# Token rows as three bf16 parts, subtracted in the banks, and gathered by three bf16 products

## The chip, the cores and the metric

The kernel runs on one core of a Trainium2 chip. The metric is the device time of one execution in microseconds (us). TensorE (PE in the profile) multiplies matrices into eight PSUM banks of 128 x 512 f32. VectorE (DVE), ScalarE (ACT) and GpSimd (POOL) do the elementwise work, and SyncE (SP) issues most of the weight transfers. The engines run side by side and wait for one another by semaphores.

## The reference, cut to what matters

One step of a two-layer encoder over 320 token rows (256 of a prompt, 64 of a sample) with 1024 features. Layer 0 mixes by an RWKV-7 recurrence, layer 1 by windowed attention, and each is followed by a mixture of 32 experts:

```
def per_sequence(t):
    lg = (t @ wg).astype(jnp.float32)                      # 4 groups
    gi = jnp.argmax(lg, axis=-1)
    ...
    tv, ti = lax.top_k(jax.nn.softmax(le, axis=-1), TOP_K) # 2 of the 8 experts of the group
    tw = tv / jnp.sum(tv, axis=-1, keepdims=True) * gp[:, None]
    ...
    gu = jnp.einsum('sd,edf->sef', t, w_gu)
    hid = jax.nn.silu(gu[..., :D_EXPERT]) * gu[..., D_EXPERT:] * cw[..., None].astype(t.dtype)
    return jnp.einsum('sef,efd->sd', hid, w_down)
```

Each token has a weight for two experts only, so 640 pairs of token and expert matter. The change is in the stage that puts the tokens in the order of their experts.

## The kernel before

The kernel is written by hand for each engine: five instruction streams, each in its written order, with a wait wherever one needs another's result. `pe.wait("mask", l)` means that TensorE waits for the instruction that another stream marked with that key. The stage before each expert loop, called the routing stage here, runs once in each layer (`moe(0)`, `moe(1)`) and has the same instructions both times:

- **TensorE** (from L986) sums the squares of the norm, makes the router's logits of the normed tokens `hT` (feature on the partition, token along the row), turns the logits and `hT` to token rows (24 transposes in f32 for `hT`, four into each of six banks: three tiles of tokens, two halves of the features), fills in with `keep_busy(9)` (products into a bank nobody reads; each f32 product is two records in the trace), waits for the mask of the chosen experts, makes the ranks with nine small bf16 products, fills in with `keep_busy(6)`, and then gathers: 16 banks (eight chunks of 128 features, two halves of 320 of the sorted places), in each three f32 products of `htok` (token rows) with `pick` (a 0/1 matrix that says which token goes to which place). After that come `keep_busy(4)` and the expert loop.
- **ScalarE** (from L1377) copies the six banks of turned tokens to `htok` (L1386, through the helper L1255). It writes them in another order of features: the 512 values of a row in the bank go out as 64 groups of 8, each of the 8 to an address 128 elements further. Then it loads the table for Exp, makes the exponentials of the router, and later copies the even chunks of the gathered rows from their banks to `xall`.
- **VectorE** (from L1710) finds group, first and second expert, builds the mask and the ranks, compares a row of numbers with each token's places (`pick`, L1812 to L1819: `is_equal`, then `is_equal` and add, in two halves of 320 places), and copies the odd chunks of the gathered rows to `xall`. When these are there, the expert loop begins.
- **GpSimd** clears the padding of the third token tile (L627), which has 64 tokens only.

PSUM banks are given out in a ring by `Banks.open`: the next bank in turn, after a wait until its last contents were read. One bank at a time can be kept out of the ring (`hold`).

The expert loop that follows takes four experts at a time. Its weights come by SyncE's queue: the first 12 MB are asked for before the routing stage, and each later one when TensorE has used up the place it goes to. The loop's last part, `scatter`, already works with three bf16 parts of each value: 48 bf16 products, each with its own 128 x 128 weights and 320 columns.

Of the kernel before, what the change touches and what calls it, by code (L numbers as in the profile page):

```python
# [31 lines left out]
BF16 = mybir.dt.bfloat16  # L32
# [4 lines left out]
P = 128  # L37
# [182 lines left out]
class Banks:  # L220


    def __init__(self, pe, ps):
        self.pe, self.ps, self.n, self.owner, self.held = pe, ps, 0, [None] * 8, None

    def hold(self, *key):

        self.held = None
        pb = self.open(*key)
        self.held = (self.n - 1) % 8  # L230
        return pb

    def open(self, *key):
        if self.n % 8 == self.held:
            self.n += 1
        b = self.n % 8
        self.n += 1
        if self.owner[b] is not None:
            self.pe.wait("read", *self.owner[b])
        self.owner[b] = key  # L240
        self.pe.seen.bank[key] = b
        return self.ps[b]


def build(nc, i, o, known, seen):
    ctx = ExitStack()
    with ctx:
# [93 lines left out]
        htok = work[:, off[0]:off[0] + 3 * D].rearrange("p (j d) -> p j d", j=3)  # L341
        hrow = htok.rearrange("p j (c q) -> p j q c", c=C)
        dpart = wk(3 * D, BF16).rearrange("p (u s d) -> p u s d", u=2, s=3)
        pick = work[:, off[0]:off[0] + 3 * ROWS].rearrange("p (j s) -> p j s", j=3)
# [11 lines left out]
        ident16 = wk(P // 2, BF16)  # L356
        triu16 = wk(P // 2, BF16)
# [237 lines left out]
        def _(eng):  # L595
# [27 lines left out]
            def cleared(l):  # L623

                pl.wait("ms ready", f"B{l}")
                eng.wait_ge(in_sems["out_written"], outs[0])
                pl.did(eng.memset(htok[64:128, 2, :], 0.0), ("htok padded", l))  # L627
# [52 lines left out]
        def _(eng):  # L680
# [26 lines left out]
            def mod_step(n):  # L707
# [3 lines left out]
                if n < MSTEPS:  # L711
                    g, c = divmod(n, C)
                    if c == 0:
                        bank.hold("mod", g)
                    eng.wait_ge(in_sems[f"modw_in{n % 2}"], 16 * (n // 2 + 1))
                    pe.did(mod_rows(ps[seen_bank(("mod", g))], c, mw[n % 2]), ("mod used", n), ("mod", g))
                elif n == MSTEPS:
                    bank.held = None
# [267 lines left out]
            def moe(l):  # L986
# [10 lines left out]
                for j, (t0, k) in enumerate(TILES):  # L997
                    for hf in range(2):
# [7 lines left out]
                        pb = bank.open("htok", l, j, hf)  # L1006
                        for cc in range(4):
                            ins = eng.transpose(pb[0:k, P * cc:P * cc + P], hT[:, 4 * hf + cc, t0:t0 + k], ident)
                        full(ins, "htok", l, j, hf)
                keep_busy(9)  # L1010
                pe.wait("mask", l)
                pb = bank.open("rank", l)
# [7 lines left out]
                keep_busy(6)  # L1020
                for hf in range(2):
                    for c in range(C):
                        pb = bank.open("rows", l, c, hf)
                        for j, (t0, kt) in enumerate(TILES):
                            if c == 0:
                                if hf == 0:
                                    pe.wait("htok ready", l, j, 1)
                                    if j == 2:
                                        pe.wait("htok padded", l)
                                pe.wait("picked", l, hf, j)  # L1030
                            ins = mm(pb[:, 0:T], htok[:, j, P * c:P * c + P], pick[:, j, T * hf:T * hf + T],
                                     j == 0, j == 2)
                        full(ins, "rows", l, c, hf)
# [212 lines left out]
        def _(eng):  # L1246
# [130 lines left out]
            def moe(l):  # L1377
# [6 lines left out]
                for j, (t0, k) in enumerate(TILES):  # L1384
                    for hf in range(2):
                        act(hrow[0:k, j, 64 * hf:64 * hf + 64, :],  # L1386
                            pk("htok", l, j, hf)[0:k, :].rearrange("p (q c) -> p q c", c=C), ACT.Copy,
                            ("read", "htok", l, j, hf), ("htok ready", l, j, hf))
# [3 lines left out]
                act(rt[:, 36, 0:3], rt[:, 35, 0:3], ACT.Exp, ("route exp", l))  # L1392
                for hf in range(2):
# [106 lines left out]
        def _(eng):  # L1500
# [209 lines left out]
            def moe(l):  # L1710
# [9 lines left out]
                op(eng.tensor_copy(ident16[:, :], cst("ident")))  # L1720
                op(eng.tensor_copy(triu16[:, :], cst("triu")))
# [313 lines left out]
```

## Time and profile before

| | us |
|---|---|
| median of 3 runs | 1304.3 (1299.38 to 1305.35) |
| the profiled execution, its own time | 1300.34 |
| its span in the trace | 1298.6 |
| gather of token rows, layer 0: first to last product | 535.10 to 561.10 |
| the same, layer 1 | 999.65 to 1025.65 |

The trace counts from the start of the span. Each row of the timeline gives the start, the length and the number of instructions that were merged into it, and in brackets how long the engine had been idle before it and what released it. A matmul in f32 is two records, in bf16 one. TensorE works 87% of the span, VectorE 42%, ScalarE 26%, and TensorE's mean granted clock is 0.949 of full speed.

### The profile page before, as it was taken

The page shows a single profiled execution, that of the slowest core. Times are in us where ns is not written, and L with a number is a line of the kernel's source. Part 1 is how long each engine was busy: PE and PEld are TensorE (multiplying, and loading weights), DVE is VectorE, ACT ScalarE, POOL GpSimd, SP SyncE. Part 2 cuts the span into 40 slices and gives each one's busy share as a digit, 9 for nine tenths or more (in the row PEclk, how much of TensorE's full clock was granted, in tenths as well). Part 3 has the DMA queues.
Part 4 walks back from the last instruction along what each step waited for, and adds up shares of the span by engine and source line. Part 5 has one row for each costly group of instructions (what it writes and reads, how often), then busy time and mean ns, then how long its engine had stood idle before and what let it go on. Part 6 is the DMA issues. An engine that isn't in the chain of part 4 may idle for free.

```text
span 1298.6 us, 22252 instructions
## 1 busy us (share of the span) xinstructions
PE 1134.0 (87%) x8975; PEld 655.4 (50%) x8975; DVE 540.4 (42%) x1419; ACT 341.0 (26%) x650; POOL 56.4 (4%) x66
## 2 busy tenths in 40 slices
PE   5579997877788879999999998899798999999985
PEld 2146665554456745644444444566575544444433
DVE  3421194424431254524444444424337244444443
ACT  1122240121111201223333323134213233333322
POOL 2000000000000000000100000000000000001000
PEclk9689998988988979999999999999798999999997
DMA  9533214877874144029999996201540099999941
GB/s 248 180 130 123 72 65 171 292 261 274 282 251 172 39 189 194 1 114 419 422 427 425 422 424 234 95 13 51 210 162 33 9 424 422 425 424 425 418 169 41
DMA packets 45971, 297.11 MB, mean 229 GB/s; under 512 B 5956, under 2 KB 7336, under 8 KB 22344
## 3 DMA queue, kind: packets, MB, share of 16 engines
q1 hardware_dynamic: 43856, 290.17, 56.4%
q0 software_dynamic: 1840, 5.79, 1.9%
q8 instruction: 58, 0.95, 0.3%
q14 instruction: 17, 0.14, 0.0%
q10 hardware_dynamic: 200, 0.06, 0.0%
HBM read 293.77 MB, written 2.24 MB: 228 GB/s over the span
## 4 chain that ended last, share of the span: by engine, by line
PE 75%; DMA 11%; DVE 8%; ACT 3%; issue 2%; SPq 0%; ACTq 0%; DVEq 0%; POOL 0%; POOLq 0%
PE bank L686 73%; DMA ring<-in_ada_w 10%; DVE work L1511 2%; ACT work L1255 2%; DMA ring<-in_kv_ada_w 1%; DVE work L1517 1%; DVE work L1514 1%; DVE rstd L1549 1%; DVE x_res L1883 1%; DMA ring<-in_rw_w_rkv 1%; PE bank L1073 1%; DVE work L1869 1%; DVE ring L1511 1%; DVE work L1623 0%; PE bank L1241 0%
## 5 line engine op out<-in xcount | busy, mean ns | idle before, releaser
L686 PE MATMUL bank<-ring,work 128*64 128x512 f32 (+1 forms) x1600 | 342.9, 582 | 9.3 <-DVE work L1869 7.6
L686 PE MATMUL bank<-work,ring 128*128 128x320 f32 (+3 forms) x1600 | 302.3, 368 | 24.6 <-DVE work L1511 8.8
L686 PEld LDWEIGHTS bank<-work,ring 128*128 128x128 f32 (+2 forms) x1600 | 214.1, 173 | 112.2 <-issue 23.9
L686 PE MATMUL bank<-work 128*128 128x320 bf16 (+7 forms) x1906 | 223.6, 283 | 20.3 <-DVE x_res L1883 7.7
L686 PEld LDWEIGHTS bank<-ring,work 128*64 128x64 f32 (+1 forms) x1600 | 113.3, 137 | 212.0 <-issue 205.0
L686 PEld LDWEIGHTS bank<-work 128*128 128x128 bf16 (+3 forms) x1906 | 164.9, 125 | 91.0 <-issue 25.1
L1255 ACT ACTIVATE work<-bank 128x320 f32<-128x320 f32 (+6 forms) x111 | 55.4, 540 | 237.1 <-PE bank L686 220.9
L686 PE MATMUL bank<-ring,cs 128*32 128x512 f32 x448 | 66.0, 680 | 49.2 <-DMA ring<-in_ada_w 42.2
L1883 DVE SCALAR_TENSOR_TENSOR x_res<-bank,mod,x_res 128x256 f32<-128x256 f32 (+1 forms) x256 | 86.2, 378 | 16.7 <-PE bank L686 2.8
L1863 DVE SCALAR_TENSOR_TENSOR work<-work,small,bank 128x256 f32<-128x256 f32 x32 | 21.5, 672 | 170.4 <-ACT work L1419 89.2
L1255 ACT ACTIVATE ring<-bank 128x512 f32<-128x512 f32 (+3 forms) x67 | 37.7, 563 | 189.9 <-PE bank L686 188.8
L686 PEld LDWEIGHTS bank<-ring 64*64 64x64 f32 (+2 forms) x1984 | 74.5, 146 | 25.4 <-issue 21.7
L686 PE MATMUL bank<-ring 64*64 64x64 f32 (+2 forms) x1984 | 84.3, 237 | 3.5 <-issue 3.5
L1876 DVE TENSOR_TENSOR work<-bank,work 128x512 f32<-128x512 f32 x64 | 44.1, 689 | 61.9 <-ACT work L1423 61.9
L640 POOL TENSOR_TENSOR work<-work 128x512 bf16<-128x512 f32 x32 | 36.4, 1160 | 539.4 <-ACT work L1427 539.4
L1423 ACT ACTIVATE work<-bank 128x512 bf16<-128x512 f32 x64 | 38.1, 596 | 49.3 <-PE bank L686 49.3
L686 PEld LDWEIGHTS bank<-ring,cs 128*32 128x32 f32 x448 | 10.3, 113 | 77.3 <-DMA ring<-in_ada_w 59.0
L1517 DVE SCALAR_TENSOR_TENSOR work<-work,vec 128x320 f32<-128x320 f32 x56 | 27.0, 548 | 52.5 <-PE bank L686 52.2
L1511 DVE TENSOR_TENSOR ring<-ring,const_phase 128x512 f32<-128x512 f32 x30 | 20.4, 679 | 58.5 <-PE bank L686 58.3
L1407 ACT COPY work<-work 128x512 f32 x64 | 39.3, 623 | 14.1 <-issue 14.1
L1427 ACT ACTIVATE work<-work 128x512 bf16<-128x512 f32 x64 | 40.1, 626 | 8.6 <-DVE work L1876 8.6
L1255 ACT ACTIVATE work<-x_res 128x640 f32<-128x640 f32 x20 | 14.7, 737 | 98.3 <-DVE x_res L1517 46.7
(189 smaller groups left out, 816.8 us busy)
## 6 DMA issues: line engine op xcount, KB each, us to landing
ring<-in_moe_w_gu SPq DMA_DIRECT2D x64, 2048.0 KB, 13.4
ring<-in_moe_w_down SPq DMA_DIRECT2D x64, 1024.0 KB, 14.2
ring<-in_ada_w SPq DMA_DIRECT2D x40, 1024.0 KB, 5.0
ring<-in_rw_w_rkv SPq DMA_DIRECT2D x6, 2048.0 KB, 7.9
ring<-in_ada_w SPq DMA_DIRECT2D x4, 2048.0 KB, 28.9
ring<-in_kv_ada_w SPq DMA_DIRECT2D x8, 1024.0 KB, 5.5
ring<-in_rw_w_o SPq DMA_DIRECT2D x2, 2048.0 KB, 11.2
ring<-in_at_w_q SPq DMA_DIRECT2D x2, 2048.0 KB, 14.1
```

What stands on the lines that cost most here:

```text
L640: eng.tensor_tensor(dpart[:, 0, 2, cols], rest[:, n, :], dpart[:, 0, 1, cols], ALU.subtract).then_inc(S["lo_ready0"], 1)
L686: return eng.matmul(out, l, r, start=start, stop=stop, **kw)
L1073: ins = eng.transpose(ps[0][:, 2 * P * u + P * f:2 * P * u + P * f + P], hid[:, u, P * f:P * f + P], ident)
L1255: ac.did(eng.activation(out, in_, f, **kw), *keys)
L1407: eng.copy(xe[:, u, :, 64 * v:64 * v + 64], xall[:, :, bass.ds(at, SLOTS)]).then_inc(S["xe_ready"], 1)
L1423: eng.activation(dpart[:, u, 0, 512 * n:512 * n + 512], ps[4 + n][:, :], ACT.Copy).then_inc(S["hi_ready"], 1)
L1427: eng.activation(dpart[:, u, 1, 512 * n:512 * n + 512], rest[:, n, :], ACT.Copy).then_inc(S["mid_ready"], 1)
L1511: op(eng.tensor_tensor(out, a, b, o_), *keys)
L1517: op(eng.scalar_tensor_tensor(out, a, s_, b, o1, o2), *keys)
L1863: eng.scalar_tensor_tensor(hid_w[:, u], silu[:, u, :].rearrange("p (q f) -> p q f", f=2), wslot[:, u:u + 1], ps[3 + 4 * u][:, FE:2 * FE].r ...
L1876: eng.tensor_tensor(rest[:, n, :], ps[4 + n][:, :], dpart[:, u, 0, 512 * n:512 * n + 512], ALU.subtract).then_inc(S["rest_ready"], 1)
L1883: ins = eng.scalar_tensor_tensor(x[:, c, t0:t0 + n], ps[(6, 1, 2)[c % 3]][:, t0:t0 + n], mod[:, l, r, 40 + c:40 + c + 1], x[:, c, t0:t0 + ...
```

## The change

The token rows are no longer kept in f32 (`htok`), but as three bf16 parts (`hpart[0..2]`) whose sum is the f32 value to the last bits. ScalarE copies each bank of turned tokens to the first part. TensorE then adds minus the part to the same bank (a product of `minus16`, minus the identity in bf16, with the part in the feature order of the bank), so that the bank holds what is left, and ScalarE copies that to the second part; once more the same for the third. The six banks stay out of the ring until the gather. `pick` is bf16, and each gathered bank is the sum of nine bf16 products (three parts, three token tiles) in place of three in f32; the products go four banks at a time, part by part.

```diff
--- before.py
+++ after.py
@@ -221,17 +221,16 @@
 
 
     def __init__(self, pe, ps):
-        self.pe, self.ps, self.n, self.owner, self.held = pe, ps, 0, [None] * 8, None
+        self.pe, self.ps, self.n, self.owner, self.held = pe, ps, 0, [None] * 8, set()
 
     def hold(self, *key):
 
-        self.held = None
         pb = self.open(*key)
-        self.held = (self.n - 1) % 8
+        self.held.add((self.n - 1) % 8)
         return pb
 
     def open(self, *key):
-        if self.n % 8 == self.held:
+        while self.n % 8 in self.held:
             self.n += 1
         b = self.n % 8
         self.n += 1
@@ -338,10 +337,12 @@
         wk(B)
         xall = wk(C * RP).rearrange("p (c s) -> p c s", c=C)
 
-        htok = work[:, off[0]:off[0] + 3 * D].rearrange("p (j d) -> p j d", j=3)
-        hrow = htok.rearrange("p j (c q) -> p j q c", c=C)
+        hpart = [t.bitcast(BF16).rearrange("p (j d) -> p j d", j=3) for t in
+                 (work[:, off[0]:off[0] + 3 * D // 2], work[:, off[0] + 3 * D // 2:off[0] + 3 * D],
+                  work[:, B:B + 3 * D // 2])]
+        hrow = [t.rearrange("p j (c q) -> p j q c", c=C) for t in hpart]
         dpart = wk(3 * D, BF16).rearrange("p (u s d) -> p u s d", u=2, s=3)
-        pick = work[:, off[0]:off[0] + 3 * ROWS].rearrange("p (j s) -> p j s", j=3)
+        pick = work[:, off[0]:off[0] + 3 * ROWS // 2].bitcast(BF16).rearrange("p (j s) -> p j s", j=3)
         rest = wk(D).rearrange("p (n d) -> p n d", n=2)
         silu = wk(2 * FE).rearrange("p (u f) -> p u f", u=2)
         hid = wk(2 * FE).rearrange("p (u f) -> p u f", u=2)
@@ -354,6 +355,7 @@
         cw = wk(3 * EXP).rearrange("p (j e) -> p j e", j=3)
         cwpart = wk(3 * 3 * EXP // 2, BF16).rearrange("p (s j e) -> p s j e", s=3, j=3)
         ident16 = wk(P // 2, BF16)
+        minus16 = wk(P // 2, BF16)
         triu16 = wk(P // 2, BF16)
         ones16 = wk(P // 2, BF16)
         msk16 = wk(3 * EXP // 2, BF16).rearrange("p (j e) -> p j e", j=3)
@@ -624,7 +626,8 @@
 
                 pl.wait("ms ready", f"B{l}")
                 eng.wait_ge(in_sems["out_written"], outs[0])
-                pl.did(eng.memset(htok[64:128, 2, :], 0.0), ("htok padded", l))
+                for t in hpart:
+                    pl.did(eng.memset(t[64:128, 2, :], 0.0), ("htok padded", l))
 
             def low_parts(l):
 
@@ -711,11 +714,12 @@
                 if n < MSTEPS:
                     g, c = divmod(n, C)
                     if c == 0:
+                        bank.held.clear()
                         bank.hold("mod", g)
                     eng.wait_ge(in_sems[f"modw_in{n % 2}"], 16 * (n // 2 + 1))
                     pe.did(mod_rows(ps[seen_bank(("mod", g))], c, mw[n % 2]), ("mod used", n), ("mod", g))
                 elif n == MSTEPS:
-                    bank.held = None
+                    bank.held.clear()
 
             def keep_busy(n):
 
@@ -1003,13 +1007,26 @@
                                 ins = eng.transpose(pb[0:k1, 36 * jj:36 * jj + 36], lgT[0:36, t1:t1 + k1],
                                                     ident[0:36, 0:36])
                             full(ins, "logits tok", l)
-                        pb = bank.open("htok", l, j, hf)
+                        pb = bank.hold("htok", l, j, hf)
                         for cc in range(4):
-                            ins = eng.transpose(pb[0:k, P * cc:P * cc + P], hT[:, 4 * hf + cc, t0:t0 + k], ident)
+                            ins = mm(pb[0:k, P * cc:P * cc + P], hT[:, 4 * hf + cc, t0:t0 + k], ident, cc == 0,
+                                     cc == 3, is_transpose=True)
                         full(ins, "htok", l, j, hf)
-                keep_busy(9)
+
+                def without(part):
+
+                    for j, (t0, k) in enumerate(TILES):
+                        for hf in range(2):
+                            pe.wait("hpart", l, part, j, hf)
+                            full(mm(ps[seen_bank(("htok", l, j, hf))][0:k, :], minus16[0:k, 0:k],
+                                    hrow[part][0:k, j, 64 * hf:64 * hf + 64, :], False, True,
+                                    skip_group_check=True), "hless", l, part, j, hf)
+
+                pe.wait("minus", l)
+                without(0)
+                keep_busy(6)
                 pe.wait("mask", l)
-                pb = bank.open("rank", l)
+                pb = bank.hold("rank", l)
                 for j in range(3):
                     for jj in range(j + 1):
                         ins = mm(pb[:, EXP * j:EXP * j + EXP], triu16[:, :] if jj == j else ones16[:, :],
@@ -1017,20 +1034,27 @@
                 for jj in range(3):
                     ins = mm(pb[:, 96:96 + EXP], ones16[:, :], msk16[:, jj, :], jj == 0, jj == 2)
                 full(ins, "rank", l)
-                keep_busy(6)
+                without(1)
+                keep_busy(3)
+                rank_bank = seen_bank(("rank", l))
+                bank.held.clear()
+                bank.held.add(rank_bank)
+                pe.wait("htok padded", l)
                 for hf in range(2):
-                    for c in range(C):
-                        pb = bank.open("rows", l, c, hf)
-                        for j, (t0, kt) in enumerate(TILES):
-                            if c == 0:
-                                if hf == 0:
-                                    pe.wait("htok ready", l, j, 1)
-                                    if j == 2:
-                                        pe.wait("htok padded", l)
-                                pe.wait("picked", l, hf, j)
-                            ins = mm(pb[:, 0:T], htok[:, j, P * c:P * c + P], pick[:, j, T * hf:T * hf + T],
-                                     j == 0, j == 2)
-                        full(ins, "rows", l, c, hf)
+                    for c4 in (0, 4):
+                        pbs = [bank.open("rows", l, c, hf) for c in range(c4, c4 + 4)]
+                        for part in range(3):
+                            for c in range(c4, c4 + 4):
+                                for j in range(3):
+                                    if c % 4 == 0:
+                                        pe.wait("hpart", l, part, j, 1)
+                                        pe.wait("picked", l, hf, j)
+                                    ins = mm(pbs[c % 4][:, 0:T], hpart[part][:, j, P * c:P * c + P],
+                                             pick[:, j, T * hf:T * hf + T], part == 0 and j == 0,
+                                             part == 2 and j == 2)
+                                if part == 2:
+                                    full(ins, "rows", l, c, hf)
+                bank.held.clear()
                 keep_busy(4)
                 pe.wait("passes", l)
                 for b in range(8):
@@ -1381,15 +1405,25 @@
                 modulated(f"B{l}", hT, hT)
                 act(lgT[0:36, :], pk("logits", l)[0:36, 0:T], ACT.Copy, ("read", "logits", l), ("logits ready", l))
                 eng.wait_ge(in_sems["out_written"], (64, 144)[l])
-                for j, (t0, k) in enumerate(TILES):
-                    for hf in range(2):
-                        act(hrow[0:k, j, 64 * hf:64 * hf + 64, :],
-                            pk("htok", l, j, hf)[0:k, :].rearrange("p (q c) -> p q c", c=C), ACT.Copy,
-                            ("read", "htok", l, j, hf), ("htok ready", l, j, hf))
+
+
+                def parts(n):
+                    for j, (t0, k) in enumerate(TILES):
+                        for hf in range(2):
+                            if n:
+                                ac.wait("hless", l, n - 1, j, hf)
+                            last = [("read", "htok", l, j, hf)] if n == 2 else []
+                            act(hrow[n][0:k, j, 64 * hf:64 * hf + 64, :],
+                                pk("htok", l, j, hf)[0:k, :].rearrange("p (q c) -> p q c", c=C), ACT.Copy,
+                                ("hpart", l, n, j, hf), *last)
+
+                parts(0)
                 ac.wait("group max", l)
                 ac.wait("top2", l)
                 act(rt[:, 6:9, 0:4], rt[:, 3:6, 0:4], ACT.Exp)
                 act(rt[:, 36, 0:3], rt[:, 35, 0:3], ACT.Exp, ("route exp", l))
+                parts(1)
+                parts(2)
                 for hf in range(2):
                     for c in range(0, C, 2):
                         act(xall[:, c, T * hf:T * hf + T], pk("rows", l, c, hf)[:, 0:T], ACT.Copy,
@@ -1718,6 +1752,7 @@
                 op(eng.memset(msk16[64:128, 2, :], 0.0))
                 op(eng.memset(before[:, 0:1], 0.0))
                 op(eng.tensor_copy(ident16[:, :], cst("ident")))
+                ts(minus16[:, :], cst("ident"), -1.0, None, M, ALU.bypass, ("minus", l))
                 op(eng.tensor_copy(triu16[:, :], cst("triu")))
                 op(eng.tensor_copy(ones16[:, :], cst("ones")))
                 eng.wait_ge(in_sems["out_written"], (64, 144)[l])
```

## Rows read from the trace of the kernel before

**Rows 1.** Page, part 1 and part 4: busy time of each engine, and the chain that ended last.
```profile
PE 1134.0 (87%) x8975; PEld 655.4 (50%) x8975; DVE 540.4 (42%) x1419; ACT 341.0 (26%) x650; POOL 56.4 (4%) x66
...
PE 75%; DMA 11%; DVE 8%; ACT 3%; issue 2%; SPq 0%; ACTq 0%; DVEq 0%; POOL 0%; POOLq 0%
```

**Rows 2.** Chain of waits, layer 0's routing stage (start us, us, what).
```profile
520.33 4.55 ACT work L1255 x5
...
525.86 1.28 ACT L1255
...
527.15 0.32 ACT work L1255 x2
...
529.86 31.26 PE bank L686 x117
...
561.14 0.49 DVE work L1834
```

**Rows 3.** Timeline, layer 0's routing stage: start us, us, engine, line, what.
```profile
509.39 0.95 POOL L627 MEMSET work<- 64x1024 f32 x1 [59.10 <-DVE rstd L1514]
...
518.49 0.22 DVE L1722 CAST work<-const 128x128 bf16<-128x128 f32 x1
...
520.33 5.51 ACT L1255 ACTIVATE work<-bank 128x512 f32<-128x512 f32 x6 [0.22 <-PE bank L1008]
...
521.04 0.23 DVE L1729 COPY work<-bank 128x72 f32<-128x72 f32 x1 [0.44 <-PE bank L1003]
...
522.67 5.01 PE L686 MATMUL bank<-const 128*128 128x320 f32 x18
...
529.86 0.39 PE L686 MATMUL bank<-work 128*128 128x32 bf16 x9 [2.18 <-DVE work L1790]
...
530.10 5.17 PE L686 MATMUL bank<-const 128*128 128x320 f32 x12
...
533.45 1.48 DVE L1517 SCALAR_TENSOR_TENSOR work<-work 128x320 f32<-128x320 f32 x3
...
535.10 26.00 PE L686 MATMUL bank<-work 128*128 128x320 f32 x96
...
536.92 0.44 ACT L1255 ACTIVATE work<-bank 128x320 f32<-128x320 f32 x1 [9.46 <-PE bank L686]
```

**Rows 4.** Groups by form, 519 to 562 us: shapes, count, busy us, mean ns.
```profile
L1255 ACT ACTIVATE work<-bank 128x512 f32<-128x512 f32 x4 | 3.7, 1085 | 0.2 <-PE bank L1008 0.2
...
L1255 ACT ACTIVATE work<-bank 64x512 f32<-64x512 f32 x2 | 2.0, 1086 | 0.0
```

**Rows 5.** Timeline, beginning and first rounds of layer 0's expert loop.
```profile
563.78 2.19 ACT L1407 COPY work<-work 128x512 f32 x4
...
588.73 0.63 ACT L1407 COPY work<-work 128x512 f32 x1 [0.20 <-issue]
...
591.10 0.60 ACT L1423 ACTIVATE work<-bank 128x512 bf16<-128x512 f32 x1 [0.43 <-PE bank L686]
...
597.86 6.69 PE L686 MATMUL bank<-work 128*128 128x320 bf16 x48
```

**Rows 6.** Timeline, layer 1's routing stage.
```profile
991.70 0.31 ACT L1255 ACTIVATE work<-work 128x12 f32<-128x12 f32 x2
...
999.65 26.00 PE L686 MATMUL bank<-work 128*128 128x320 f32 x96
```

**Rows 7.** Windows of 1 us: share of busy time (instructions) of each engine, TensorE's granted clock, DMA.
```profile
531.00:532.00 1.00, 1.00 (x4) 0.72 (x3) 0.90 (x6) 0.00 (x0) 0.00 (x0) 0.64 0.00 0
532.00:533.00 1.00, 1.00 (x3) 0.61 (x3) 0.93 (x5) 0.00 (x0) 0.00 (x0) 0.50 0.00 0
533.00:534.00 1.00, 1.00 (x4) 0.61 (x3) 0.96 (x4) 0.00 (x0) 0.00 (x0) 0.50 0.00 0
534.00:535.00 1.00, 1.00 (x4) 0.72 (x3) 1.00 (x3) 0.00 (x0) 0.00 (x0) 0.65 0.00 0
535.00:536.00 1.00, 1.00 (x5) 0.68 (x5) 0.96 (x4) 0.00 (x0) 0.00 (x0) 1.00 0.00 0
```

## The prediction

> **What bounds the kernel now.** I read the page first: TensorE is busy 87% of the span, and three quarters of the chain that ended last are its own [rows 1]. A faster gather on TensorE can therefore pay, if nothing else comes to stand before it. Next the chain of waits through the routing stage of layer 0 [rows 2]: ScalarE's copies of the turned tokens, its table load and its exponentials lead to the mask, and from 529.86 the chain stays on TensorE for 31.26 us, until VectorE copies the last gathered bank at 561.14. Of these 31.26 us the gather is 26.00 (535.10 to 561.10), 96 records for 48 f32 products [rows 3]. Layer 1 has the same 26.00 us, from 999.65 [rows 6]. What follows (fillers, VectorE's selection, the expert loop) hangs on the gather's end. The refills of the loop's weights are asked for when TensorE has used a place up, so they move with it; the first 12 MB were asked for before this stage, and the window rows show the transfers silent here [rows 7]. So what the end of the gather gains or loses is gained or lost by the program, twice.
>
> When can the gather begin? Before, with the last `pick` of its first half: VectorE's compare-and-add ends at 534.93 [rows 3], and the first product starts at 535.10. The fillers ahead of it end there too, since TensorE's clock was at half in part of this stretch [rows 7]. ScalarE has nothing to do from its exponentials (527.47) to 536.92 [rows 2, 3]. This gap is what the change uses.
>
> **The gather's products.** 144 bf16 products of 320 columns take the place of 48 in f32. The nearest rows are those of the loop's scatter: the same shape, each with its own 128 x 128 weights, 48 in 6.69 us [rows 5], so 0.139 us each. 144 x 0.139 = 20.1 us against 26.0: 5.9 us less in each layer. Bounds: below, 320 columns cannot be had for less than the record of an f32 product costs per column (26.00 / 96 = 0.271 us for two passes, so 0.135 and 19.5 us); above, if a step from bank to bank every three products cost something that scatter (six to a bank) does not show, I allow 0.15 and 21.6 us. I take 0.139.
>
> **The parts on ScalarE.** Before there are six copies from bank to `htok`, 5.51 us in all, one 1.09 us long [rows 3, 4]; so the start of each follows the last one's by (5.51 - 1.09) / 5 = 0.88 us. A copy of as many values to consecutive addresses takes 0.60 us [rows 5], so the scattered order (groups of eight, 128 elements apart) costs 0.49. The first part's six copies stay where they are. Twelve more come behind the exponentials, which end at 527.15 + 0.32 = 527.47 [rows 2]. Each writes bf16 in the same scattered order. No row has that. From below: the pace of consecutive writes, (2.19 - 0.63) / 3 = 0.52 us [rows 5]; from above: twice the pace now, 1.77, if a two-byte write to a place of its own costs more than a four-byte one. I take 0.88, since the addresses are as scattered as before and bf16 to consecutive addresses costs no more or less than f32 [rows 5].
>
> The Trainium skill (ScalarE: Activation LUTs, What ACT_TABLE_LOAD costs) gives an ACTIVATE with immediate operands as 186 ns + 0.833 ns a column for fp32 and bf16 alike, which is 613 ns for 512. The trace agrees for consecutive writes (0.60) and not for scattered ones (1.09). By the page ten copies would be done after some 5.3 us, and the gather would wait for `pick` as before.
>
> How many of the twelve stand before the gather? The six banks are held, and `rows` opens four banks before its first product. In the ring's order from the first held bank: two `htok` banks, the logits' bank (taken by `rank`, still held), four `htok` banks, one free. The first four opened are thus the `htok` banks of tiles 0 and 1, and each waits until its third part was read. So the gather begins with the tenth of the twelve copies: 527.47 + 9 x 0.88 + 1.09 = 536.5, with 0.05 for the semaphore 536.55. That is 1.45 later than before. The last two copies (to 538.3) are needed only by the third part, after 24 products or 3.3 us (539.9): hidden. Later groups of four find banks read long before, the nearest being chunk 0's, full nine products (1.25 us) before its group ends against a copy of 0.44.
>
> **TensorE between.** The six subtractions of the first part follow ScalarE's copies at their pace and end soon after 525.84; then six fillers (12 records at 5.01 / 18 = 0.28) until 529.5. TensorE goes on with the mask at 529.86 [rows 3]. The next six subtractions stand behind `rank` (530.25) and follow the copies of the second part, the last at some 532.9; three fillers, to 534.8. All before 536.5, hidden with 1.7 us to spare. If this cover goes, each microsecond costs one.
>
> **The rest, at nothing.** `minus16` is one VectorE instruction (0.22) before a stretch in which VectorE waits 0.44 in layer 0 [rows 3]. Three GpSimd memsets for one of 0.95 at 509.39 end by 512.3, more than 20 us before their wait. `pick` in bf16: same instructions over 320 columns; should they be slower, 1.6 us lie between 534.93 and 536.5. ScalarE's new waits for the second and third part have the Exp of the router ahead of them, not behind, and behind them only the even chunks of the gather, which come later. No DMA is added or moved.
>
> **The sum.** Layer 0's gather ends at 536.55 + 20.1 = 556.65, against 561.10: 4.45 less. In layer 1 the exponentials end at 992.01 [rows 6], and the same steps give 1001.1 + 20.1 = 1021.2 against 1025.65: 4.45. Together 8.9 us. The profiled execution took 1300.34 (span 1298.6 and 1.7 around it), so it becomes 1291.4. The median of the three runs is 4.0 above that execution, with nothing to tell the two kernels apart in this, so I take the loss from the median: 1304.3 - 8.9 = 1295.4.
>
> **Rivals.**
> - **Clock.** TensorE was granted half its clock (1.2 GHz) from 531.3 to 534.7, after it had stood idle for 2.18 us before `rank`; the four windows add up to 1.7 us of lost work [rows 7], now hidden behind `pick`. With the change TensorE has thin work from 530 to 533 (six subtractions) and nothing from 534.8 to 536.5. If such a stretch falls on the gather, each costs 1.7 us. One in each layer: 8.9 - 3.4 = 5.5 us, 1298.8, hardly told from no change.
> - **Fast scattered bf16.** ScalarE's copies at the pace of consecutive writes: the gather begins with `pick` at 535.0 and the gain is 5.9 - 0.0 in each layer, 11.8: 1292.5.
> - **Slow reads on TensorE.** The subtraction's moving operand is the part in scattered order, 256 bytes from one value to the next. No row has such a read. If it went at ScalarE's scattered pace (0.88 us for 512), the second set would end at 530.25 + 5.3 = 535.5, the fillers at 537.2: 0.65 lost in each layer, gain 7.6, 1296.7. At twice that, the set would end at 540.9, the gather would begin at 542.5, and the program would be 3 us slower. The Trainium skill (SBUF — State Buffer, Door 1: The DMA port swizzle, its note on cachelines) says that each access that crosses to a new 16-byte line pays; by it these reads pay at every value, which is why this rival has a chance of its own. No row here shows the size of it.
> - **Slow scattered bf16 (slower).** ScalarE's twelve copies at 1.77: the tenth ends at 527.47 + 9 x 1.77 + 2.2 = 545.6, the gather 20.1 later at 565.7: 4.6 more than before in each layer, 9 together, 1313.5. It decides from a pace of 0.88 + 4.45 / 9 = 1.37 us. For it speaks only that the order already costs 0.49; against it, that nothing suggests a price by width.
> - **The gather not faster than its row.** The break-even is (26.0 - 1.45) / 144 = 0.170 us a product; scatter's 0.139 leaves room.
>
> **How the numbers follow.** The sum as it stands 0.47 (own range 1292 to 1299), the clock 0.20, fast copies 0.12, slow reads at 0.88 0.07, slower than before by either of the two scattered accesses 0.12, products too slow 0.02. A measurement of this kernel tells some 0.5%, 6.5 us. Faster by more: the sum, but for its upper end, fast copies and part of slow reads, 0.57; within: the clock and those ends, 0.31; slower 0.12. The range leaves out the slower cases and the luckiest of the fast ones: 1289 to 1304.
>
> **What would show it.** In the trace after: twelve ScalarE copies 128x512 bf16 from 527.4 with starts 0.88 apart; TensorE's first bf16 product of 320 columns some 1.4 us later against the exponentials than now, released by ScalarE; 144 of them in 20.1 us; full clock from there on. Wrong would be: copies more than 1.37 apart, subtractions longer than 0.9, a granted clock under 1 in the gather, or a wait within it.

## The result and the profile after

The changed kernel takes 1344.91 us (median of 4 runs, 1340.24 to 1348.19) where the kernel before takes 1302.38 (4 runs): a ratio of 1.0324, 95% interval 1.0282 to 1.0366. The forecast was 1295.4, with a range to 1304. It is slower by 42.5 us, and the rival that ended on this side, slow scattered bf16, had the right place at less than a quarter of its size.

The page of the changed kernel, part 1 and part 4, to lay beside [rows 1]:

```profile
PE 1150.3 (86%) x9071; PEld 650.7 (49%) x9071; DVE 540.7 (40%) x1421; ACT 413.1 (31%) x674; POOL 59.9 (4%) x70
...
PE 71%; DMA 12%; DVE 8%; ACT 7%; issue 2%; SPq 0%; ACTq 0%; DVEq 0%; POOL 0%; POOLq 0%
```

ScalarE has 24 more instructions and 72 us more work: 24 new copies at a pace of 2.27 us, and the first part's twelve, six in each layer, each 1.39 slower than before. Its share of the chain rose from 3% to 7%. The chain of waits through layer 0's routing stage says where:

```profile
522.48 4.56 ACT work L1279 x2
527.03 1.96 issue
528.99 7.31 ACT work L1279 x3
...
536.32 1.28 ACT L1279
...
537.61 23.10 ACT work L1279 x12
...
560.95 21.27 PE bank L689 x144
```

From 522.48 to 537.61 + 23.10 = 560.71 the chain is ScalarE's alone (the last twelve pieces are two exponentials and ten copies); before, it left ScalarE at 527.47 [rows 2]. The timeline, to lay beside [rows 3]:

```profile
522.48 13.82 ACT L1279 ACTIVATE work<-bank 128x512 bf16<-128x512 f32 x6 [0.22 <-PE bank L689]
...
527.27 1.02 PE L689 MATMUL bank<-work 128*128 128x512 bf16 x1 [1.16 <-ACT work L1279]
...
529.54 1.02 PE L689 MATMUL bank<-work 128*128 128x512 bf16 x1 [1.25 <-ACT work L1279]
...
537.83 27.42 ACT L1279 ACTIVATE work<-bank 128x512 bf16<-128x512 f32 x12
...
538.02 0.17 DVE L1804 TENSOR_REDUCE work<-work 128x3 f32<-128x12 f32 x1 [10.29 <-ACT work L1279]
```

The subtractions start 2.27 us apart, each released by a copy: that is ScalarE's pace, where the forecast had 0.88. The first six copies take 13.82 us in place of 5.51, and VectorE waits 10.29 us for the exponentials behind them. The groups by form give one copy's length, to lay beside [rows 4]:

```profile
L1279 ACT ACTIVATE work<-bank 128x512 bf16<-128x512 f32 x12 | 28.1, 2713 | 0.2 <-PE bank L689 0.2
L689 PE MATMUL bank<-work 128*128 128x320 bf16 x144 | 21.3, 313 | 4.7 <-ACT work L1279 4.7
```

2.71 us where the same 512 values as f32 in the same order took 1.09. The stage in its three steps, in us, layer 0:

| | before | forecast | after |
|---|---|---|---|
| first copy to the end of the exponentials | 7.1 | 7.1 | 15.4 |
| from there to the gather's first product | 7.6 | 9.1 | 23.0 |
| the gather | 26.0 | 20.1 | 21.3 |

The stage lasts 59.7 us instead of 40.8 (18.9 more); in layer 1, where the gather takes 22.5, 20.3 more. Together 39.2 of the 39.9 us between the two profiled executions (1340.24 and 1300.34).

### The profile page after: what moved, and what is told of

It reads as the page before. It is cut to its first block, busy times and chain, and to the rows that moved or that the text cites. A ratio compares the mean times of both kernels' runs of the same rounds, so it can differ in the third digit from the quotient of the medians.

```text
span 1338.5 us, 22484 instructions
## 1 busy us (share of the span) xinstructions
PE 1150.3 (86%) x9071; PEld 650.7 (49%) x9071; DVE 540.7 (40%) x1421; ACT 413.1 (31%) x674; POOL 59.9 (4%) x70
## 4 chain that ended last, share of the span: by engine, by line
PE 71%; DMA 12%; DVE 8%; ACT 7%; issue 2%; SPq 0%; ACTq 0%; DVEq 0%; POOL 0%; POOLq 0%
PE bank L689 69%; DMA ring<-in_ada_w 9%; ACT work L1279 6%; DVE work L1545 2%; DMA ring<-in_kv_ada_w 2%; DVE work L1551 1%; DVE work L1548 1%; DVE rstd L1583 1%; DVE x_res L1918 1%; DMA ring<-in_rw_w_rkv 1%; PE bank L1097 1%; DVE work L1904 1%; DVE ring L1545 1%; DVE work L1657 0%; PE bank L1265 0%
## 5 line engine op out<-in xcount | busy, mean ns | idle before, releaser
L689 PE MATMUL bank<-work,ring 128*128 128x320 f32 (+3 forms) x1600 | 305.5, 371 | 24.3 <-DVE work L1545 8.7
L689 PE MATMUL bank<-work 128*128 128x320 bf16 (+8 forms) x2026 | 240.1, 283 | 45.6 <-ACT work L1279 30.8
L689 PEld LDWEIGHTS bank<-work,ring 128*128 128x128 f32 (+2 forms) x1600 | 216.9, 175 | 112.3 <-issue 25.1
L689 PEld LDWEIGHTS bank<-work 128*128 128x128 bf16 (+2 forms) x2026 | 161.9, 117 | 134.2 <-ACT work L1279 40.4
L1279 ACT ACTIVATE work<-bank 128x320 f32<-128x320 f32 (+7 forms) x135 | 127.6, 1076 | 210.6 <-PE bank L689 195.0
L1279 ACT ACTIVATE work<-x_res 128x640 f32<-128x640 f32 x20 | 14.7, 736 | 99.6 <-DVE x_res L1551 46.7
```

Source lines behind the costliest of these rows:

```text
L689: return eng.matmul(out, l, r, start=start, stop=stop, **kw)
L1279: ac.did(eng.activation(out, in_, f, **kw), *keys)
```

## The experiments

**Everything in the bank's order.** All three parts are written and read back in the bank's own order in place of the scattered one. This kernel leaves out the reordering of the features, and its instructions are otherwise the same:

```diff
-        hrow = [t.rearrange("p j (c q) -> p j q c", c=C) for t in hpart]
+        hrow = [t.rearrange("p j (q c) -> p j q c", c=C) for t in hpart]
```

> The three parts are written and read back in the bank's own feature order (512 bf16 in a row), nothing else is changed; the order of the features in the gathered rows is then another, which leaves part of the computation wrong and every duration as it would be. Theory (the order of the two-byte writes costs ScalarE 2.27 us instead of 0.88 a copy, and with it all of the loss): copies drop to 0.50 to 0.53 us apart, subtractions from 1.02 to 0.22 us, the gather starts when the first half of the row picks is there, about 7.5 us behind the exponentials, and the program takes 1289 to 1294 us. Rival (the copies are slow because they read a bank that TensorE adds to, or because they round to bf16, whatever the order): copies stay at 2.27 us and the time at 1340 to 1348.

Measured: 1286.1 us, ratio 0.9887 (0.9817 to 0.9956), 3 us under the range that was expected. Its timeline in layer 0:

```profile
525.70 3.27 ACT L1279 ACTIVATE work<-bank 128x512 bf16<-128x512 f32 x6 [0.22 <-PE bank L689]
...
534.93 3.01 ACT L1279 ACTIVATE work<-bank 128x512 bf16<-128x512 f32 x6 [0.16 <-PE bank L689]
...
538.56 0.68 PE L689 MATMUL bank<-work 128*128 128x320 bf16 x2 [0.65 <-DVE work L1551]
539.39 19.46 PE L689 MATMUL bank<-work 128*128 128x320 bf16 x142 [0.15 <-DVE work L1551]
```

Same engine, same banks, same rounding to bf16, and six copies in 3.27 us instead of 13.82: the order of the addresses is the cause, and the rival (the bank, or the rounding) falls. The gather now waits for VectorE's `pick`, that of the first token tile, and its products run at 19.46 / 142 = 0.137 us.

**ScalarE in order, TensorE scattered.** The subtraction alone reads with 64 elements between its values:

```diff
+        hnat = [t.rearrange("p j (q c) -> p j q c", c=C) for t in hpart]
...
-                                    hrow[part][0:k, j, 64 * hf:64 * hf + 64, :], False, True,
+                                    hpart[part][0:k, j, 512 * hf:512 * hf + 512].rearrange("p (c q) -> p q c", c=C), False, True,
...
-                            act(hrow[n][0:k, j, 64 * hf:64 * hf + 64, :],
+                            act(hnat[n][0:k, j, 64 * hf:64 * hf + 64, :],
```

> ScalarE writes the parts in the bank's order, TensorE's subtraction still reads in scattered order (128 bytes from one value to the next), so what is subtracted belongs to another feature and the parts and outputs are wrong by that. If ScalarE's writes are the whole loss: near 1292, the gather held up only by the second set of subtractions, 6 x 1.02 behind the ranks and three fillers, about 3 us later than in the run in bank order, in each layer: 1296 to 1300. If TensorE's scattered reads were the bound: copies would wait for them and the time would stay above 1320.

Measured: 1302.91 in a single run, 17 us above the run in bank order and more than expected. TensorE's timeline, and two windows of 1 us with its granted clock in the third column from the right:

```profile
524.34 5.41 PE L690 MATMUL bank<-work 128*128 128x512 bf16 x6
529.68 5.12 PE L690 MATMUL bank<-const 128*128 128x320 f32 x12
534.64 5.64 PE L690 MATMUL bank<-work 128*128 128x32 bf16 x15
540.21 3.36 PE L690 MATMUL bank<-const 128*128 128x320 f32 x6
543.40 19.72 PE L690 MATMUL bank<-work 128*128 128x320 bf16 x144
```

```profile
531.00:532.00 1.00, 1.00 (x4) 0.60 (x3) 0.69 (x3) 0.06 (x1) 0.00 (x0) 0.50 0.00 0
...
541.00:542.00 1.00, 1.00 (x4) 0.61 (x3) 0.96 (x7) 0.00 (x0) 0.00 (x0) 0.50 0.00 0
```

The expectation priced only the second set of six. Here the first set (5.41 us) also pushes back the fillers, and the ranks begin at 534.64, though the mask was there at 530.54. The fillers themselves run at half clock: it falls at the end of each of the two scattered sets, although TensorE had not been idle, and the twelve and the six records take 5.12 and 3.36 us where the run in bank order, at full clock throughout, has 3.50 and 1.88. TensorE's queue is one line, so each scattered set delays all that stands behind it. From the first copy to the gather's end the stage takes 41.1 us in layer 0 and 43.0 in layer 1, against 33.2 in the run in bank order: 17.8 us together, which bears out the single time. With fast copies the subtraction's reads cost the whole gain.

**ScalarE scattered, TensorE in order.** The counterpart:

```diff
-                                    hrow[part][0:k, j, 64 * hf:64 * hf + 64, :], False, True,
+                                    hpart[part][0:k, j, 512 * hf:512 * hf + 512], False, True,
...
-                            act(hrow[n][0:k, j, 64 * hf:64 * hf + 64, :],
+                            act(hpart[n][0:k, j, 512 * hf:512 * hf + 512].rearrange("p (c q) -> p q c", c=C),
```

> The counterpart of the second run: ScalarE writes the parts in scattered order (64 elements between values), TensorE's subtraction reads them in a row, so what is subtracted belongs to another feature and parts and outputs are wrong by that. If ScalarE's copies at 2.27 us set the gather's start alone in the changed kernel, TensorE's reads lie beside them: subtractions fall from 1.02 to 0.38 us or so and the time stays at 1336 to 1346. If the reads had a share of their own on top, the time falls by their share, 17 us between the first two runs, to about 1327.

Measured: 1343.18 in a single run. One subtraction and the next in its trace:

```profile
529.63 0.39 PE L689 MATMUL bank<-work 128*128 128x512 bf16 x1 [1.81 <-ACT work L1279]
531.91 0.39 PE L689 MATMUL bank<-work 128*128 128x512 bf16 x1 [1.89 <-ACT work L1279]
```

The subtraction's record falls from 1.02 to 0.39 us, its pace stays ScalarE's, and the program gains nothing that a run can tell. So the two scattered accesses do not add: 1286 with neither, 1303 with TensorE's, 1343 with ScalarE's, 1345 with both. In the changed kernel ScalarE's writes are the whole loss, and they hide TensorE's reads.

**Prices by distance.** The kernel before, with copies and products of 512 values added in layer 0's routing stage. A first run had all of ScalarE's under one line of the helper. Its copies at a distance of 64, `s4` being f32 and `s2` bf16:

```diff
+                    act(s4.rearrange("p (a b) -> p b a", b=64), const[:, 0:512].rearrange("p (b a) -> p b a", b=64), ACT.Copy)
+                    act(s2.rearrange("p (a b) -> p b a", b=64), const[:, 0:512].rearrange("p (b a) -> p b a", b=64), ACT.Copy)
```

> The kernel before, with copies of 512 f32 values of a constant to spare space added in layer 0's routing stage, first to f32 and then to bf16, with 1, 2, 4, 8, 16 and 64 elements from one written value to the next on ScalarE (VectorE: 1, 8 and 64), and bf16 products of 512 columns on TensorE whose moving values lie 1 to 64 elements apart. Theory (a two-byte write that does not go beside its neighbour costs by its own, more than a four-byte one): on ScalarE f32 goes from 0.63 to about 1.1 us and bf16 from 0.63 to about 2.7 us at 64; the step shows at which distance it begins. Rival (the bank is the cause): bf16 from this source stays below 1.1 us at every distance. TensorE: 0.22 us a product at 1, 1.02 at 64.

Measured: ScalarE's twelve copies in 16.33 us together, which the mixed group cannot divide; VectorE at a distance of 64 took 1.35 us for bf16 and 0.63 for f32. Since the source was a constant and not a bank, the average of 1.36 already speaks against the rival. The second run gave each access its own line, and added runs of values:

> As the run with strides, each access with a line of its own in the trace, and with runs: 1, 2, 4, 8 or 32 values beside each other, then a jump. If it is the single two-byte write that costs (2.3 to 2.7 us for 512), runs of two bf16 (four bytes) should fall to the price of scattered f32 (1.1) or under it, and runs of 4 or more to about 0.6. If it is the jump itself, runs of two halve the price at both widths and the two-byte ones stay dearest. TensorE's scattered moving values: 1.02 us at a distance of 64, near 0.5 in runs of two, 0.22 to 0.3 in runs of 8.

ScalarE's timeline, in this order: f32 side by side; bf16 at distances of 1, 2, 4, 8 and 64 elements; f32 at 2, 4 and 64; bf16 in runs of 2 and of 4, each run 64 from the next:

```profile
534.29 0.61 ACT L1419 ACTIVATE work<-const 128x512 f32<-128x512 f32 x1
534.93 0.63 ACT L1421 ACTIVATE work<-const 128x512 bf16<-128x512 f32 x1
535.59 0.77 ACT L1423 ACTIVATE work<-const 128x512 bf16<-128x512 f32 x1
536.40 1.35 ACT L1425 ACTIVATE work<-const 128x512 bf16<-128x512 f32 x1
537.78 2.50 ACT L1427 ACTIVATE work<-const 128x512 bf16<-128x512 f32 x1
540.31 2.53 ACT L1429 ACTIVATE work<-const 128x512 bf16<-128x512 f32 x1
542.87 0.69 ACT L1431 ACTIVATE work<-const 128x512 f32<-128x512 f32 x1
543.59 1.15 ACT L1433 ACTIVATE work<-const 128x512 f32<-128x512 f32 x1
544.78 1.12 ACT L1435 ACTIVATE work<-const 128x512 f32<-128x512 f32 x1
545.92 0.67 ACT L1437 ACTIVATE work<-const 128x512 bf16<-128x512 f32 x1
546.63 0.63 ACT L1439 ACTIVATE work<-const 128x512 bf16<-128x512 f32 x1
```

Both widths rise with the distance until a value has 16 bytes to itself (8 bf16, 4 f32), and no further at 64: f32 to 1.15, bf16 to 2.53. Two bf16 side by side, the same four bytes as one f32, cost 0.67. So it is neither the jump nor the rounding alone, but the single two-byte write away from its neighbours. The Trainium skill (SBUF — State Buffer, Door 1: The DMA port swizzle, its note on cachelines) speaks of 16-byte lines and calls strides up to 4 fp32 or 8 bf16 free. These rows agree that the price stops rising once each value has 16 bytes to itself, but not that shorter strides are free: bf16 at a distance of 4 (8 bytes) already took 1.35 us against 0.63.

TensorE had each product twice in a row, and the time from start to start is the pace: moving bf16 values at a distance of 1, at 64, in runs of 2 and in runs of 4. Behind it VectorE's bf16 copies at 64 and in runs of 2:

```profile
569.07 0.38 PE L1039 MATMUL bank<-const,work 128*128 128x512 bf16 x1
569.29 0.38 PE L1040 MATMUL bank<-const,work 128*128 128x512 bf16 x1
...
572.64 1.04 PE L1047 MATMUL bank<-const,work 128*128 128x512 bf16 x1
573.50 1.04 PE L1048 MATMUL bank<-const,work 128*128 128x512 bf16 x1
574.37 0.61 PE L1049 MATMUL bank<-const,work 128*128 128x512 bf16 x1
574.80 0.61 PE L1050 MATMUL bank<-const,work 128*128 128x512 bf16 x1
575.23 0.40 PE L1051 MATMUL bank<-const,work 128*128 128x512 bf16 x1
575.47 0.38 PE L1052 MATMUL bank<-const,work 128*128 128x512 bf16 x1
```

```profile
546.63 1.32 DVE L1889 CAST work<-const 128x512 bf16<-128x512 f32 x1
547.99 0.43 DVE L1891 CAST work<-const 128x512 bf16<-128x512 f32 x1
```

TensorE's paces are 0.22, 0.86, 0.43 and 0.24 us. VectorE pays threefold for single values, ScalarE fourfold.

**Fillers up to the gather.** In the changed kernel:

```diff
-                keep_busy(3)
+                keep_busy(12)
```

> The changed kernel with twelve fillers in place of three before the gather, so that TensorE has no idle stretch there while it waits for ScalarE's third part. If the half clock at the gather's start follows from that idle stretch, the gather takes 19.6 us instead of 21.3 and 22.5: 4 to 5 us less in all, about 1340 against 1345. If not, the gather stays at 21 to 23 us. ScalarE's copies stay 2.27 us apart, so the loss as a whole stays.

Measured: the gather takes 19.74 us in layer 0 and 19.79 in layer 1, against 21.27 and 22.53. First the windows of the changed kernel, then of this run, with TensorE's granted clock in the third column from the right:

```profile
560.00:561.00 1.00, 0.05 (x1) 0.08 (x2) 0.00 (x0) 1.00 (x2) 0.00 (x0) 0.50 0.00 0
...
563.00:564.00 1.00, 1.00 (x5) 0.59 (x4) 0.00 (x0) 1.00 (x1) 0.00 (x0) 0.50 0.00 0
564.00:565.00 1.00, 1.00 (x9) 0.67 (x7) 0.00 (x0) 1.00 (x1) 0.00 (x0) 0.95 0.00 0
```

```profile
562.00:563.00 1.00, 1.00 (x7) 0.60 (x7) 0.00 (x0) 1.00 (x1) 0.00 (x0) 1.00 0.00 0
```

After 4.74 us without a product the gather began at 1.2 GHz; with fillers ahead of it, at 2.4 GHz. So half clock costs the two gathers 4.3 us. The fillers do not give all of that back: they end after the banks are free, and the gather starts 23.9 and 23.8 us behind the exponentials instead of 23.0 and 23.1, which leaves some 2.6 us. The time of the single run, 1341.6, is 3.3 under the changed kernel's median, but within the spread of its runs.

**The bank in the gather's order.** The transposes spread their values over the bank, so that everything after them goes by runs of 64:

```diff
-        hrow = [t.rearrange("p j (c q) -> p j q c", c=C) for t in hpart]
+        hrow = [t.rearrange("p j (c q) -> p j c q", c=C) for t in hpart]
...
-                            ins = mm(pb[0:k, P * cc:P * cc + P], hT[:, 4 * hf + cc, t0:t0 + k], ident, cc == 0,
+                            ins = mm(pb[0:k, :].rearrange("p (c q) -> p q c", c=C)[:, 16 * cc:16 * cc + 16, :],
+                                     hT[:, 4 * hf + cc, t0:t0 + k], ident, cc == 0,
...
-                                    hrow[part][0:k, j, 64 * hf:64 * hf + 64, :], False, True,
+                                    hrow[part][0:k, j, :, 64 * hf:64 * hf + 64], False, True,
...
-                            act(hrow[n][0:k, j, 64 * hf:64 * hf + 64, :],
-                                pk("htok", l, j, hf)[0:k, :].rearrange("p (q c) -> p q c", c=C), ACT.Copy,
+                            act(hrow[n][0:k, j, :, 64 * hf:64 * hf + 64],
+                                pk("htok", l, j, hf)[0:k, :].rearrange("p (c q) -> p c q", c=C), ACT.Copy,
```

> As the changed kernel, but TensorE's transposes write each bank in the order that the gather needs (eight runs of 64 features; a value 256 bytes from the next), so that ScalarE and the subtraction go by runs of 64. Everything is computed. Theory: copies 0.50 to 0.55 us apart, subtractions 0.22; the 24 transposes are at worst as slow as scattered reads (about 1 us more for a bank's four, 6 in each layer, partly beside ScalarE): 1289 to 1300. Rival (the order of the transposes' writes costs as much as it did on ScalarE): 2 us a bank, over 1310.

Measured: 1289.75 us, ratio 0.9881 (0.9811 to 0.9950), faster than both kernels with all of the computation. Its timeline:

```profile
526.65 1.97 PE L689 MATMUL bank<-const,work 128*128 128x128 f32 x16
527.34 2.04 ACT L1280 ACTIVATE work<-bank 128x512 bf16<-128x512 f32 x4
...
530.69 1.28 ACT L1280 ACT_TABLE_LOAD   x1 [1.31 <-DVE work L1546]
...
539.80 19.46 PE L689 MATMUL bank<-work 128*128 128x320 bf16 x142 [0.15 <-DVE work L1552]
```

The transposes take 1.97 us for 16 records as in the changed kernel (1.96): their scattered writes to the bank cost nothing. ScalarE's copies are as fast as in bank order.

**The gather's weights scattered.** The first run's parts, and in the gather

```diff
+        hcol = [t.rearrange("p j (q c) -> p j c q", c=C) for t in hpart]
...
-                                    ins = mm(pbs[c % 4][:, 0:T], hpart[part][:, j, P * c:P * c + P],
+                                    ins = mm(pbs[c % 4][:, 0:T], hcol[part][:, j, c, :],
```

> Parts in the bank's order as in the first run, but the gather takes its weights with 8 elements (16 bytes) between values, so that everything is computed. ScalarE and the subtractions as there (0.50 and 0.22 us). If scattered reads cost the weight load as they cost the moving operand (1.02 us for 512, so 0.25 for 128 columns against a product of 0.136), the gather's 144 products go at some 0.25 us, 36 us: about 1318. If the load stays hidden beside the product before it: 1286 to 1292.

Measured: 1288.9 in a single run. The gather takes 20.35 us for its 144 products, the wait for `pick` in it included, against 20.30 with weights side by side (first to last product of the version before); the weight loads are longer (0.144 us mean against 0.098) and still beside the products. The price of the moving operand does not carry over to the weights here, but no room is left either: within the gather the weight load is busy all of the time, against 72% in the run in bank order. Whether shorter products would still hide it is not shown.

**The table of Exp early**, one `act(small[:, 12:13], small[:, 12:13], ACT.Exp)` behind `parts(0)`, on top of the bank in the gather's order.

> The version whose transposes write the bank in chunk order, with one Exp of a spare value directly behind the first part, so that ScalarE loads the table of Exp while it would wait for VectorE's second expert (1.31 us idle, then 1.28 us of loading, in the trace of that version). With that version the gather starts when VectorE's picks are ready, and these follow from the exponentials: each layer should end its gather 1.2 to 1.3 us sooner, so 2.5 us less than that version, near 1287, and 15 to 20 us (1.2 to 1.5%) less than the kernel before.

Measured: 1288.61 us, ratio 0.9872 (0.9840 to 0.9905):

```profile
532.49 1.28 ACT L1280 ACT_TABLE_LOAD   x1
```

The idle 1.31 us ahead of the load is gone, and from the logits' copy to the gather's end layer 0 takes 32.8 us against 33.8. The runs do not tell it from the version without (1289.75).

**The order alone.** The kernel before, f32 throughout, with the transposes and copies of the version above.

> The kernel before, f32 parts and products untouched, with only the transposes writing each bank in the order that the gather needs, so that ScalarE's six f32 copies go by runs of 64. This tells what the order alone is worth, without the three bf16 parts: copies 0.50 to 0.53 us apart instead of 0.88, the exponentials 0.9 us sooner in each layer, the gather's 26.0 us unchanged: 1.8 us less, not to be told from the kernel before (ratio 0.995 to 1.002). If the order were worth most of what the version with both gained, the ratio would be 0.99.

Measured: 1298.99, ratio 0.9988 (0.9962 to 1.0015): no change that can be told. Its trace has the six copies in 3.27 us (5.51 before), from the logits' copy to the exponentials' end 6.85 us (7.79), and this around the gather, to lay beside [rows 3]:

```profile
533.10 3.48 PE L686 MATMUL bank<-const 128*128 128x320 f32 x12
537.06 26.11 PE L686 MATMUL bank<-work 128*128 128x320 f32 x96 [0.48 <-DVE work L1518]
```

The twelve filler records take 3.48 us where they took 5.17 at half clock, and the gather, now released by VectorE's `pick`, starts 6.6 us behind the exponentials instead of 7.6. From the logits' copy to the gather's end each layer takes 39.6 us, against 41.4 before and 33.8 in the version with bf16 parts in the same order. So of the 7.6 us that this version gains in a layer, 1.9 come with the order and 5.7 with the bf16 products; the 1.9 are too few for the runs to tell.

## Why the prediction was wrong

**Failed: the price of a copy in scattered bf16.** "I take 0.88, since the addresses are as scattered as before and bf16 to consecutive addresses costs no more or less than f32." Both halves of that reason hold, and the conclusion does not: width and order were each priced alone, and it is their product that costs. Measured: 2.27 us apart, in both layers, past the 1.37 that the forecast named as the pace that decides. The upper bound of 1.77 was twice the known pace with no row behind the factor; it lay below the truth, and so did the range (to 1304) and the slow rival's 1313.5.

**Failed: "The first part's six copies stay where they are."** They stay in the queue, but they change width too, and they stand ahead of the exponentials: 13.82 us for 5.51, 8.3 us a layer that neither the sum nor the slow rival had. With sixteen copies ahead of the gather's start instead of ten, 16 x (2.27 - 0.88) = 22.2 us and the 1.45 of the forecast make 23.7; the first two steps of the table rose by 38.4 - 14.7 = 23.7.

**Right: the place where the gather hangs.** It starts with the tenth of the twelve copies: the chain has the tenth end at 560.71, and the first product is at 560.95. Four held banks, opened before the first product, make that wait.

**Right in kind, hidden here: slow reads on TensorE.** Its guess of 0.88 us for 512 agrees with the measured 0.86 to 0.90. In the changed kernel ScalarE's copies cover it. Behind fast copies it cost 17 us, not the 1.3 worked out (0.65 a layer), because the first set and the fillers behind it, at half clock, delayed the ranks as well.

**Right: the products.** 0.139 forecast, 0.136 to 0.137 at full clock.

**Half right: the clock rival.** It priced 1.7 us a layer; half clock cost the gathers 1.5 and 2.7, and the run with fillers took that away. But the idle stretch ahead of it, 4.74 us, is made by the slow copies. With fast copies and subtractions in order (the run in bank order) the granted clock was 1.00 in every window from the mask to the gather, so thin work alone did not bring the rival about; behind fast copies and scattered subtractions the clock did fall.

**Misread: what released the gather before.** The forecast has it start with the last `pick` of its first half, with the fillers ending there too. The kernel waits for the `pick` of one token tile at a time, and that of the first was done at 534.0, the first product at 535.1. It was the fillers, at half clock, that held the gather: with them at full clock it starts 6.6 to 6.7 us behind the exponentials instead of 7.6. That is 1 us a layer that the sum did not see.

**Right: the rest at nothing.** `minus16`, the three memsets (done by 996.3 in layer 1) and `pick` in bf16 (1.48 us for three instructions, as before) stay hidden.

**The sum itself** is low rather than high when the order is mended. With fast copies the forecast had 11.8 us less; the two versions that compute everything and were timed several times measured 1.2% and 1.3% less, 15.5 and 15.25 us between the medians. The interval of the first includes 11.8, that of the second, which also has the early table, begins at 12.4. The trace of the first accounts for its 15.5: from the logits' copy to the gather's end each layer takes 33.8 us instead of 41.4. Of these 7.6 us the gather is 5.7 (20.3 for 26.0), the exponentials are 0.9 sooner, and the gather starts 1.0 sooner behind them.

## What to carry to other kernels

Price a copy by width and order together: a row for the same order at another width, or the same width in another order, is not a row for it. When an instruction that stays in place changes its type, everything queued behind it is part of the change, here the exponentials. And put a reordering where it is free: on the transposes' way into PSUM or on the weights' side of products of 320 columns it cost nothing, on ScalarE's bf16 writes it cost 57 us (1343 against 1286).

## What the runs showed of the hardware

- A scattered write of single bf16 values costs ScalarE 2.53 us for 512 and VectorE 1.32, against 1.12 and 0.61 for f32 in the same order and 0.63 and 0.43 side by side; in runs of two it is 0.67 and 0.43.
- TensorE's moving bf16 values take 0.86 to 0.90 us for 512 when 8 or more elements apart, 0.43 in runs of two; its weights at 8 elements apart took 0.144 us a load instead of 0.098, which products of 320 columns (0.136) still hid.
- Transposes that wrote f32 to a bank with 64 elements between neighbours took as long as side by side: 1.97 us for 16 records.
- Six products in a row with scattered moving values, 5.41 us without an idle stretch, were followed by a granted clock of 0.50 (1.2 GHz) for 3 us in layer 0 and 6 in layer 1; the same six with values side by side were not.
